# Second mixer: the order of weight splits, head norms and head outputs on three engines

## What is computed

```python
def _mixer(h, lb, w_in, b_in, a_q_g, a_k_g, b_conv_w, out_g, w_out):
    z = h @ w_in + b_in
    (a_q, a_k, a_v, a_f, b_qk, b_v, b_i, b_f, b_o, c_q, c_f, c_i, c_g) = _split_cols(z)
    qa = _rms(_heads(a_q, A_HEADS), a_q_g)                 # 8 heads of 64
    ka = _rms(_heads(a_k, A_HEADS), a_k_g)
    ca = jnp.cumsum(jax.nn.log_sigmoid(a_f.astype(f32)), axis=1).transpose(0, 2, 1)
    oa = _fox_attention(qa, ka, _heads(a_v, A_HEADS), ca)  # softmax with a forget gate
    qk = jax.nn.silu(_causal_dwconv(b_qk, b_conv_w))       # 4 taps
    ...
    ob = _mlstm_chunkwise(...)                             # 4 heads of 64
    logf = jnp.logaddexp(jnp.log(lbh), jnp.log1p(-lbh) + jax.nn.log_sigmoid(_heads(c_f, C_HEADS)))
    oc = _hgrn2_chunkwise(jax.nn.silu(_heads(c_q, C_HEADS)), logf, _heads(c_i, C_HEADS))  # 4 heads
    ya = _rms(_merge(oa), ...)
    yb = jax.nn.sigmoid(b_o.astype(f32)) * _rms(_merge(ob), ...)
    yc = jax.nn.silu(c_g.astype(f32)) * _rms(_merge(oc), ...)
    return jnp.concatenate([ya, yb, yc], axis=-1).astype(h.dtype) @ w_out
```

## Time and profile before

| | before |
|---|---|
| median of 3 runs | 1839.66 us |
| lowest, highest | 1839.43, 1841.38 us |
| the profiled execution | 1839.02 us |
| its span, first to last instruction | 1837.1 us |
| PE busy | 1793.1 us, 98% of the span |
| DVE busy | 1404.6 us, 76% |
| ACT busy | 1131.6 us, 62% |
| mean granted clock of TensorE | 0.99 |

### The profile page before, as it was taken

How to read it: one execution, slowest core, us unless ns; L and a number is a source line. 1 busy time by engine, 2 the same in 40 slices (tenths; PEclk the granted TensorE clock), 3 DMA queues, 4 the chain that set the end, 5 groups by cost and what they waited for, 6 DMA issues and landing times.

```text
span 1837.1 us, 25790 instructions
## 1 busy us (share of the span) xinstructions
PE 1793.1 (98%) x10004; PEld 1551.9 (84%) x10004; DVE 1404.6 (76%) x1164; ACT 1131.6 (62%) x942; POOL 116.8 (6%) x133
## 2 busy tenths in 40 slices
PE   7999999999999999999999999999999999899999
PEld 6889999998888888888888888888888797789998
DVE  6475445555888988889889889898898868777775
ACT  6444434463677777777777767767777634645553
POOL 7000000000000000000000000000000018400000
PEclk9999999999999999999999999999999999989999
DMA  7446565532898998998999989989989644315561
GB/s 235 161 140 205 167 201 184 165 133 81 323 383 324 374 377 310 388 371 322 378 345 356 373 313 390 370 322 381 370 330 369 220 133 138 115 63 190 184 200 53
DMA packets 244356, 479.27 MB, mean 261 GB/s; under 512 B 11759, under 2 KB 80137, under 8 KB 244249
## 3 DMA queue, kind: packets, MB, share of 16 engines
q1 hardware_dynamic: 243385, 476.43, 72.6%
q10 hardware_dynamic: 864, 1.31, 0.2%
HBM read 476.66 MB, written 1.05 MB: 260 GB/s over the span
## 4 chain that ended last, share of the span: by engine, by line
PE 90%; DVE 5%; ACT 2%; POOL 1%; issue 1%; DMA 0%; DVEq 0%; ACTq 0%; SPq 0%; POOLq 0%
PE bank L1976 28%; PE bank L1978 27%; PE bank L1977 27%; PE bank L2286 2%; PE bank L2318 1%; DVE wl L438 1%; PE bank L1945 1%; POOL arena L821 1%; DVE xT L1292 0%; DVE xTl L1235 0%; POOL arena L820 0%; PE bank L2355 0%; PE bank L2356 0%; ACT wh L431 0%; PE bank L1955 0%
## 5 line engine op out<-in xcount | busy, mean ns | idle before, releaser
L1976 PE MATMUL bank<-wh,xTh 128*128 128x512 f32 x1568 | 620.3, 396 | 5.2 <-DVE wl L438 2.8
L1978 PE MATMUL bank<-wh,xTl 128*128 128x512 f32 x1568 | 611.7, 390 | 0.0
L1977 PE MATMUL bank<-wl,xTh 128*128 128x512 f32 x1568 | 610.7, 390 | 0.0
L1539 DVE TENSOR_TENSOR wl<-raw,wh 128x2048 fp32r<-128x2048 f32 x224 | 512.2, 2291 | 92.5 <-ACT wh L1024 90.8
L1024 ACT ACTIVATE wh<-raw 128x2048 fp32r<-128x2048 f32 x224 | 429.1, 1917 | 120.7 <-PE bank L1978 120.7
L1976 PEld LDWEIGHTS bank<-wh,xTh 128*128 128x128 f32 x1568 | 294.9, 188 | 67.1 <-DVE wl L438 3.7
L1978 PEld LDWEIGHTS bank<-wh,xTl 128*128 128x128 f32 x1568 | 294.6, 188 | 62.6
L1977 PEld LDWEIGHTS bank<-wl,xTh 128*128 128x128 f32 x1568 | 295.1, 188 | 58.5
L438 DVE TENSOR_TENSOR wl<-raw,wh 128x2048 fp32r<-128x2048 f32 x112 | 254.7, 2291 | 72.1 <-ACT wh L431 70.4
L1976 PE MATMUL bank<-xTh,wh 128*128 128x256 f32 x1024 | 290.8, 284 | 5.0 <-DVE wl L438 3.7
L1978 PE MATMUL bank<-xTh,wl 128*128 128x256 f32 x1024 | 289.7, 283 | 0.0
(11 more groups left out here) (379 smaller groups left out, 1406.4 us busy)
## 6 DMA issues: line engine op xcount, KB each, us to landing
raw<-in_moe_w_up SPq DMA_DIRECT2D x112, 1024.0 KB, 7.6
arena<-in_moe_w_gate SPq DMA_DIRECT2D x96, 1024.0 KB, 7.4
raw<-in_moe_w_down SPq DMA_DIRECT2D x96, 1024.0 KB, 7.0
raw<-in_w_up SPq DMA_DIRECT2D x22, 1024.0 KB, 5.6
raw<-in_moe_w_gate SPq DMA_DIRECT2D x16, 1024.0 KB, 7.7
arena<-in_moe_w_down SPq DMA_DIRECT2D x16, 1024.0 KB, 7.7
raw<-in_gla_w_in SPq DMA_DIRECT2D x12, 1024.0 KB, 7.6
raw<-in_w_in SPq DMA_DIRECT2D x12, 1024.0 KB, 6.1
```

Of the source, the lines that this page charges most:

```text
L1539: V.tensor_tensor(wl[:, s, :], moe_raw(c)[0], wh[:, s, :].bitcast(F32), ALU.subtract).then_inc(lo_moe, 1)
L1976: T.matmul(o, xh, yh, start=first, stop=False)
L1977: T.matmul(o, xh, yl, start=False, stop=False)
L1978: return T.matmul(o, xl, yh, start=False, stop=last)
```

## The change

It touches no arithmetic; the same instructions are issued, on the same engines, in another order and with other banks. Five parts:

1. ACT casts both `aq` pieces ahead of the gates of the recurrent heads, and DVE splits `aq` and the first `bqk` piece there, and one piece more at the next such place.
2. `qkss` moves one level on, behind `av` of the second tile; ACT's logarithms move from `ahead(6)` to `ahead(7)`. The banks of these results shift, and bvo1 and `cross` get banks 6, 7 and 5 by hand.
3. On ACT the casts of pieces `w2` 2 and 3 leave the fox heads: one stands behind them, the other behind the mLSTM exponentials. The split of the fox outputs' transposes goes ahead of the gates (1205).
4. On DVE `fox_out` and its mean squares go ahead of the exponents, on ACT the squares ahead of the exponentials and `head_rstd` between them; `Dm` gets four buffers in place of two.
5. On PE the last two heads' values go ahead of the mLSTM scores, with `mT` between them.

```diff
-            turn(("bvo", 1))
+            turn(("bvo", 1), 6)
             for g in range(cross):
-                turn((pre, P, g))
+                turn((pre, P, g), 7 - 2 * g)
...
-                     5: [("av", 0), "qkss"], 6: [("av", 1)], 7: [("bvo", 0)]}
+                     5: [("av", 0)], 6: [("av", 1), "qkss"], 7: [("bvo", 0)]}
...
-        Dm = ar(2 * 384).rearrange("p (a n) -> p a n", a=2)
+        Dm = ar(4 * 384).rearrange("p (a n) -> p a n", a=4)
...
+            hi.upto(pos["aq", 1])
             gone(act, ("cqf", 0))
...
-                if i == 6:
+                if i == 7:
                     for k in range(4):
                         A(V.activation(rs[:, k * 512:(k + 1) * 512], see(act, ("qkss", k))[:, :], ACT.Ln, scale=1.0 / HD,
                                        bias=c_eps), frees=("qkss", k))
-                if i == 7:
                     for k in range(2):
...
-                if hd == 1:
-                    hi.upto(pos[("w2", 0), 1])
...
-                if hd == 3:
-                    hi.upto(pos[("w2", 1), 1])
+            hi.upto(pos[("w2", 0), 1])
...
+            act.wait_ge(sg("o_fox"), 1)
+            A(V.activation(osq[:, 0:TT * AD].rearrange("p (t n) -> p t n", t=TT), o_all[:, :, 0:AD], ACT.Square), "o_sq")
+            for hd in range(2):
+                decay(hd)
             head_rstd(0, 24, 1)
+            for hd in range(2, BH):
+                decay(hd)
+            hi.upto(pos[("w2", 1), 1])
+            split_x(quarters("yy", True)[0:2])
...
-            split_x(quarters("yy", True)[0:2])
...
-            lo.upto(pos["aq", 1])
+            lo.upto(pos["bqk", 0])
...
-            lo.upto(pos["bqk", 0])
+            lo.upto(pos["bqk", 1])
...
+            fox_out()
             exponents(0)
             exponents(1)
-            fox_out()
+            dve.wait_ge(sg("o_sq"), 1)
+            mean_squares(0, osq[:, 0:TT * AD], AH)
+            tick("hs_ready")
             weighted(0)
             exponents(2)
             weighted(1)
-            exponents(3)
-            dve.wait_ge(sg("o_sq"), 1)
-            mean_squares(0, osq[:, 0:TT * AD], AH)
-            tick("hs_ready")
             dve.wait_ge(sg("hs_rstd"), 1)
             scaled(o_all[:, :, 0:AD], 0, AH)
             tick("o_a")
+            exponents(3)
...
+            fox_values(AH - 2)
             pe.wait_ge(sg("m_rows"), 1)
...
+            fox_values(AH - 1)
...
-            lstm_scores(0)
-            for hd in (AH - 2, AH - 1):
-                fox_values(hd)
-            lstm_scores(1)
+            for b in range(BH // 2):
+                lstm_scores(b)
```

More of the change, by code:

```diff
@@ L1192, in head_rstd, with decay @@
                 A(V.activation(rstd[:, c0:c0 + n], rstd[:, c0:c0 + n], ACT.Exp, scale=-0.5), "hs_rstd")
-            for hd in range(BH):
+            def decay(hd):
                 gone(act, ("P2", hd))
                 for st in range(TT):
-                    sl = Dm[:, hd % 2, 0:S] if st == 0 else Dm[:, hd % 2, S:384]
+                    sl = Dm[:, hd, 0:S] if st == 0 else Dm[:, hd, S:384]
                     A(V.activation(sl, sl, ACT.Exp, bias=iT[:, st * BH + hd:st * BH + hd + 1]), "d_exp")
-                if hd == 1:
-                    act.wait_ge(sg("o_fox"), 1)
-                    A(V.activation(osq[:, 0:TT * AD].rearrange("p (t n) -> p t n", t=TT), o_all[:, :, 0:AD], ACT.Square), "o_sq")
+            act.wait_ge(sg("o_fox"), 1)
+            A(V.activation(osq[:, 0:TT * AD].rearrange("p (t n) -> p t n", t=TT), o_all[:, :, 0:AD], ACT.Square), "o_sq")
+            for hd in range(2):
+                decay(hd)
             head_rstd(0, 24, 1)
+            for hd in range(2, BH):
+                decay(hd)
+            hi.upto(pos[("w2", 1), 1])
+            split_x(quarters("yy", True)[0:2])
             for t in range(TT):
@@ L1858, in exponents @@
             def exponents(hd):
-                C(V.tensor_tensor(Dm[:, hd % 2, :], see(dve, ("P2", hd))[:, 0:384], c3, ALU.add), frees=("P2", hd))
+                C(V.tensor_tensor(Dm[:, hd, :], see(dve, ("P2", hd))[:, 0:384], c3, ALU.add), frees=("P2", hd))
             def scaled(a, c0, n):
@@ L1871, in weighted @@
                 dve.wait_ge(sg("d_exp"), TT * (hd + 1))
-                C(V.scalar_tensor_tensor(sS[:, hd % 4, :], p1, HD ** -0.5, Dm[:, hd % 2, :], ALU.mult, ALU.mult), frees=("P1", hd))
+                C(V.scalar_tensor_tensor(sS[:, hd % 4, :], p1, HD ** -0.5, Dm[:, hd, :], ALU.mult, ALU.mult), frees=("P1", hd))
+            fox_out()
             exponents(0)
             exponents(1)
-            fox_out()
+            dve.wait_ge(sg("o_sq"), 1)
+            mean_squares(0, osq[:, 0:TT * AD], AH)
+            tick("hs_ready")
             weighted(0)
@@ L1886, in _ @@
             tick("o_a")
+            exponents(3)
+            evac("yy", [(xT, "out_g_2", 0)], None, order(True)[0:1])
             weighted(2)
-            evac("yy", [(xT, "out_g_2", 0)], None, order(True)[0:1])
+            evac("yy", [(xT, "out_g_2", 0)], None, order(True)[1:2])
             weighted(3)
-            evac("yy", [(xT, "out_g_2", 0)], None, order(True)[1:2])
             split_x("yy", quarters("yy", True), [0, 1])
```

## The result

The changed kernel takes 1842.83 us (median of 20 runs), the kernel before 1839.76 us (20 runs): a ratio of 1.0018, with a 95% interval of 1.0012 to 1.0024. That is 3.1 us slower, where 1.9 us faster was forecast, and 1.0 us above the end of the range.

A forecast was written before the change was run, and what follows sets the result against it. The prediction took PE, on the chain for 90% of the span, as the bound, its pauses and slow clock costing some 20 us. Terms 0.2 - 3.5 + 1.0 + 0.4 = -1.9 us gave 1837.8 us, range 1833.4 to 1841.8.

The forecast's parts named there:

- The three waits: Second mixer: PE's three waits for DVE's weight splits, 3.7 us in all, were to go.
- Term 1: Up to the fox scores: the savings ahead are given back by bvo1's wait and slow clock, +0.2 us.
- Term 2: Fox heads, fox scores to fox_out: fewer casts on ACT, slow clock again behind the seventh head, -3.5 us.
- rival (a): Fox heads: the stage keeps its full clock, -6.1 us there, sum -4.5, 1835.2 us; chance 0.20.
- fox_out to the transposes: From fox_out to the fox outputs' transposes: stays about equal to the 7.65 us before.
- Term 3: Transposes to out projection: one more decay and a cast on ACT, 5.2 us in place of 4.18, +1.0 us.
- The prediction's own sign for this term: Between transposes and out projection: a split following o_a by 4 us or less would show the +1.0 us wrong.
- Term 4: Out projection: it starts at the lower clock, losing 2.0 us in place of 1.6, +0.4 us.
- (c): Ahead of bvo1: the pause keeps the clock at half into the fox scores, +2.7 to +5.4 us; chance 0.10.
- (d): Whole change: the stall and the cast in front of the split eat all gain, 0, 1839.7 us; chance 0.07.

The follow-up runs named there:

- e1: Kernel before with only the weight casts and splits moved ahead of the gates: 1836.94 us, ratio 0.9980 to the kernel before.
- e6: Changed kernel with bvo1 in bank 3 in place of bank 6: 1839.27 us, ratio 0.9993 to the kernel before.
- e2: Kernel before with only qkss and the logarithms one level on and the new banks for bvo1 and cross: 1844.77 us, ratio 1.0023.
- e3: Kernel before with only the w2 casts moved, fox_out ahead of the exponents and the last heads' values ahead: 1840.17 us, ratio 0.9999.
- e8: Changed kernel with bvo1 in bank 3, POOL's last split waiting for DVE's transpose splits, and fox transposes in banks 3 and 4: 1836.31 us.
- e9: Changed kernel with qkss, logarithms and bvo1/cross banks as before, POOL's last split behind DVE's transpose splits, fox transposes in banks 3 and 4: 1837.44 us.
- e12: Changed kernel with bvo1 in bank 3, fox transposes in banks 3 and 4 and both last casts behind the fox heads: 1834.33 us.
- e5: Changed kernel with one wait added, so POOL's last split begins only after DVE's splits of the fox transposes: 1843.92 us.
- e10: Changed kernel with both last w2 casts behind the fox heads, none ahead of the split of the transposes: 1838.76 us.
- e11: Changed kernel with qkss, logarithms and bvo1/cross banks as before, fox transposes in banks 3 and 4, both last casts behind the fox heads: 1832.53 us.

## Why the prediction was wrong

**The first part held.** The three waits went, as forecast, and alone the part is worth 3.7 us (e1).

**Term 1, +0.2 forecast, +1.2 measured: right mechanism, size off.** POOL's chain in the changed kernel, its first convolution and last sum, and one of its operations beside the last weight split on DVE:

```profile
1515.99 0.94 POOL L818 TENSOR_SCALAR arena<-arena,vT 128x256 f32<-128x256 f32 x1 [1.69 <-ACT arena L1125]
...
1555.92 2.84 POOL L820 TENSOR_SCALAR arena<-arena,vT 128x253 f32<-128x253 f32 x1
...
1560.38 0.63 POOL L762 TENSOR_TENSOR arena<-arena 128x256 f32<-128x256 f32 x1
```

```profile
1555.28 2.70 DVE L438 TENSOR_TENSOR wl<-raw,wh 128x2048 fp32r<-128x2048 f32 x1
```

It starts 2.75 us earlier behind `cig`, as forecast (2.8), but lasts 45.0 us instead of 43.3, where 44.2 was forecast. The sums end 1.0 us earlier and not 1.9. The six POOL operations that a weight split stretches lose 1.6 to 2.3 us each, 11.8 in all, where 11.2 were taken; that is inside the ends given. So 0.9 of the 1.0 us that this term is off is POOL's chain. From there on the chain through ACT was forecast almost exactly, 8.35 us from the end of the sums to the half of the addition; 8.4 was measured:

```profile
1561.09 0.42 ACT L862 ACTIVATE arena<-arena 128x256 f32<-128x256 f32 x1 [9.27 <-POOL arena L762]
...
1561.99 2.85 ACT L1146 ACTIVATE rs_home<-bank,cst 128x512 f32<-128x512 f32 x4
1564.87 2.14 ACT L1149 ACTIVATE rs_home<-rs_home 128x1024 f32<-128x1024 f32 x2
1567.04 0.42 ACT L862 ACTIVATE arena<-arena 128x256 f32<-128x256 f32 x1
```

The logarithms stand where ACT waited for POOL anyway before, and now behind that wait. bvo1 waits 5.42 us (about 5 forecast), and the slow clock takes 2.3 us from it (7.95 us from its start to `cross` in place of 5.67; 1.9 forecast). That is 0.4 more than forecast, and `cross` takes back 0.15. What I named correctly, the bank, is worth 3.6 us (e6). Having found it, the text should have gone one step further: this part alone makes the kernel slower (e2), and only the first part's gain covers it.

**Term 2, -3.5 us, held**: 23.35 against 26.85, with the clock at 1.2 GHz again behind the seventh head, as forecast and against rival (a). That it came out to the tenth is partly luck: from the fox scores to the end of the last copy it gave 1.9 us, where the text had 2.0 to 2.7, and from there to `fox_out` 1.6 in place of 1.1; alone (e3) the same parts gave 4.7.

**fox_out to the transposes, forecast unchanged, +1.3 us: a step that was missing.** I looked at who computes the scaled outputs and not at the banks of the transposes. They have banks 0 and 1, and those hold the last head's P2 and the third's P1. exponents(3) has moved behind `o_a`, so bank 0 comes free later, and weighted(2) keeps bank 1: the two waits of 1.25 and 1.54 us. With banks 3 and 4, which are free earlier, the stage is 8.3 us and the transposes run in one go (e8, e9, e12). That is 0.7 of the 1.3 us. The other 0.65 is in DVE's order: the scaled outputs themselves come that much later behind `fox_out`. ACT's `head_rstd` is ready at 1606.95, but DVE does three operations on the exponents and weighted values first:

```profile
1606.73 0.22 ACT L1189 ACTIVATE rstd<-rstd 128x24 f32<-128x24 f32 x1
```

```profile
1608.10 1.22 DVE L1867 TENSOR_TENSOR xn<-xn,rstd 128x1024 f32<-128x1024 f32 x1
```

The prediction named ACT's exponentials ahead of `head_rstd`; it had left out DVE's work behind it.

**Term 3, +1.0 forecast, +3.9 measured: the step that failed.** The prediction saw the cast ahead of the split on ACT:

```profile
1611.17 1.91 ACT L431 ACTIVATE wh<-raw 128x2048 fp32r<-128x2048 f32 x1
1612.98 0.61 ACT L842 ACTIVATE xTh<-xT 128x512 fp32r<-128x512 f32 x1
```

But of what the cast triggers it said that POOL's splits come later and the second half of the out projection alone uses them. The user of the result was harmless; the operation itself was not. It starts at 1613.15, and DVE's two splits, 1.42 us if undisturbed, take 4.03 us beside it. The stretching of POOL beside DVE was in the prediction, priced as 10.3 us of POOL's chain from the earlier trace rows; that the same conflict stops DVE when POOL is first was not thought of. The Trainium skill, "SBUF — State Buffer", section "SBUF: two separate sides", says that whichever of the two starts first holds the shared port pair for its whole instruction and the other blocks. The two rows of e9, 4.57 us on POOL and 4.44 us on DVE, agree. The 3.9 us come apart by the runs. Keeping POOL's split away from DVE's takes 1.6 away (e5: 6.45). Moving the cast as well takes 0.45 more (e10: 6.00), so the cast on ACT, the one cost that the prediction had here, at 1.0, was the small one. The banks take nearly all of the rest: 1.6 between e5 and e8 (4.88), 1.6 and 1.9 between e10 and e12 (4.39) or e11 (4.14). So what failed is the sum of this step, a cast and one exponential: the block of DVE by POOL and the banks of the transposes were not in it at all. The prediction's own sign for this term, a split 4 us or less behind `o_a`, did show: ACT's split began 3.5 us behind the mark at 1609.51. It was meant to show a term too large, and the term was too small.

**Term 4** was +0.4 and is +0.3.

Of the rivals, the sign was that of (c), but not its mechanism: bvo1's slow clock ended at 1574.2 and didn't reach the fox scores. (d) had the cast in front of the split eat the gain, but only down to zero. No rival had POOL's split or the banks of the transposes in the stretch between the fox outputs and the out projection, where 5.2 us were lost (1.3 + 3.9), 1.0 of it forecast.

## What to carry to other kernels

When a cast or a copy is moved, price the operations that it triggers on other engines at their new place too: not only who waits for their results, but what runs beside them, and in both directions, DVE stopped by POOL as well as POOL by DVE. Delaying such an operation by a semaphore only moved the collision here; it was better to start it where the other engine reads PSUM. When work is put in another order, list for every PSUM bank who held it last: the wait ahead of bvo1 and both waits ahead of the transposes are a bank given to a result whose last reader comes late in the new order. When several parts are put into one change, price each alone: part 2 cost 4.2 us and the splits hid it.

## What the runs showed of the hardware

- A POOL operation of 128x2048 elements (4.5 us) stops a DVE operation with both inputs in SBUF, even a tiny one: two of 128x512 took 4.03 us instead of 1.42, one of 128x4 took 4.44 (e9; 4.45 in e5, 4.43 in e8) instead of 0.16. DVE operations with one input in PSUM ran through it at their usual 0.69 and 0.56 us, and in e10 one with a single input, in SBUF, at its usual 1.22.
- A large DVE split started beside a POOL operation was itself stretched, to 2.70 us from 2.29 (changed kernel).
- After PE had stood 5.4 us its clock stayed at 1.2 GHz for 4.8 us of full work. Matmuls on the identity in the pauses ahead of the out projection held it at 2.4 GHz (1.00 against 0.61 and 0.53).
